# LayerNorm of a conformer convolution on eight Trainium2 cores: all spreads made at once, statistics in four row groups, residuals queued behind part of the next tile's normalisation, second projection's weight loads behind the relayout

## What is computed

```python
def conv_module(h, state, w_pw1, b_pw1, w_dw, b_dw, ln_g, ln_b, w_pw2, b_pw2):
    a, gt = jnp.split(h @ w_pw1 + b_pw1, 2, axis=-1)
    u = a * jax.nn.sigmoid(gt)                                   # GLU (B, T, D)
    up = jnp.concatenate([state.astype(u.dtype), u], axis=1)
    z = lax.conv_general_dilated(up, w_dw[:, None, :], ...) + b_dw
    z = jax.nn.silu(layer_norm(z, ln_g, ln_b))
    return z @ w_pw2 + b_pw2, up[:, T:]
...
x = x + g1[:, None, :] * y
h = modulate(rms_norm(x, p['norm_ffn'][i]), sh2, sc2)
```

## Time and profile before

| what | us |
|---|---|
| median of 3 runs (3391.39 to 3393.15) | 3391.57 |
| the profiled execution | 3392.49 |
| its span on the slowest core (core 5) | 3391.4 |
| spans of the eight cores | 3371.2 to 3391.4 |
| TensorE busy on core 5 | 3085.2 |

### The profile page before, as it was taken

One profiled execution on the slowest core, in us unless ns is written; L12 is line 12 of the kernel. 1 busy time (PEld: TensorE's weight loads), 2 busy tenths in 40 slices (PEclk: granted clock), 3 DMA queues, 4 the chain that ended last, 5 costly groups with the idle time before them and its releaser, 6 DMA issues.

```text
span 3391.4 us, 54958 instructions; the slowest of 8 cores (3371.2 to 3391.4 us)
## 1 busy us (share of the span) xinstructions
PE 3085.2 (91%) x22054; PEld 1831.1 (54%) x22054; DVE 1158.1 (34%) x2470; ACT 671.8 (20%) x1587; POOL 271.2 (8%) x391
## 2 busy tenths in 40 slices
PE   1299995797999999999999889989899999999997
PEld 0055552444555555555555445556566666666664
DVE  0543334424142213141222636652414414141417
ACT  1222223323000000000001546641300000000013
POOL 0000001001000000000000122410100000000000
PEclk9599996898999999999999999999899999999999
DMA  9956764244777877777752231214343444444443
GB/s 194 191 110 133 140 130 94 86 75 75 125 125 127 142 127 127 125 125 125 127 95 52 41 73 36 57 26 75 53 74 68 81 75 75 75 73 73 72 73 113
DMA packets 78139, 327.71 MB, mean 97 GB/s; under 512 B 19825, under 2 KB 39153, under 8 KB 43697
## 3 DMA queue, kind: packets, MB, share of 16 engines
q0 software_dynamic: 40432, 283.66, 47.7%
q1 hardware_dynamic: 37458, 40.54, 4.1%
HBM read 593.07 MB, written 10.19 MB: 178 GB/s over the span
## 4 chain that ended last, share of the span: by engine, by line
PE 85%; DVE 5%; DMA 3%; ACT 3%; issue 2%; SPq 2%; another core or an unknown queue 1%; POOL 0%; DVEq 0%; ACTq 0%; POOLq 0%
PE ps L308 85%; SPq L303 2%; DVE X L314 1%; DVE SCR L314 1%; ACT HB L311 1%; DMA X<-xT 1%; DVE X L317 1%; ACT SCR L311 1%; DVE SCR L681 1%; DMA RING<-wgu 1%; DMA UBraw<-UBraw 1%; POOL HB L693 0%; DMA kT_o<-UBraw 0%; DMA RING<-wpw 0%
## 5 line engine op out<-in xcount | busy, mean ns | idle before, releaser
L308 PE MATMUL ps<-HB,RING 128*128 128x384 bf16 (+2 forms) x11712 | 1946.0, 327 | 81.9 <-DVE X L317 20.7
L308 PEld LDWEIGHTS ps<-HB,RING 128*128 128x128 bf16 x11712 | 1140.4, 99 | 852.8 <-issue 159.5
L308 PE MATMUL ps<-UBraw,RING 128*128 128x384 bf16 (+3 forms) x5248 | 814.0, 313 | 1.8 <-DVE AMB L317 0.8
L308 PEld LDWEIGHTS ps<-UBraw,RING 128*128 128x128 bf16 x5248 | 492.7, 98 | 301.6 <-issue 19.2
L317 DVE SCALAR_TENSOR_TENSOR X<-ps,MOD,X 128x16 f32<-128x16 f32 (+2 forms) x1120 | 454.9, 447 | 469.9 <-PE ps L308 466.8
L314 DVE TENSOR_TENSOR UBraw<-ps,SCR 128x384 bf16<-128x384 f32 (+2 forms) x264 | 144.2, 547 | 1184.0 <-PE ps L308 1177.8
L311 ACT ACTIVATE SCR<-ps 128x416 f32<-128x416 f32 (+4 forms) x336 | 169.0, 504 | 1782.0 <-PE ps L308 1759.8
L311 ACT ACTIVATE SCR<-X 128x384 bf16<-128x384 f32 (+3 forms) x224 | 135.9, 609 | 260.0 <-DVE X L317 257.3
L308 PE MATMUL ps<-SCR,ONESB 128*128 128x384 bf16 (+3 forms) x336 | 87.7, 357 | 76.9 <-ACT SCR L311 73.1
L127 POOL DMA_DIRECT2D RING<-wgu x88 | 46.8, 531 | 1169.5 <-PE ps L308 1169.4
L311 ACT ACTIVATE SCR<-ps,UBraw 128x193 bf16<-128x193 f32 (+1 forms) x264 | 109.1, 419 | 90.7 <-DVE UBraw L1263 41.5
(11 more groups left out here) (91 smaller groups left out, 1058.9 us busy)
## 6 DMA issues: line engine op xcount, KB each, us to landing
RING<-wmod POOLq DMA_DIRECT2D x96, 1024.0 KB, 15.4
RING<-wgu POOLq DMA_DIRECT2D x88, 1024.0 KB, 8.9
RING<-wdn POOLq DMA_DIRECT2D x40, 1024.0 KB, 8.6
RING<-wpw POOLq DMA_DIRECT2D x24, 1024.0 KB, 15.4
RING<-wqkv POOLq DMA_DIRECT2D x10, 1024.0 KB, 9.0
X<-xT SPq DMA_DIRECT2D x4, 2368.0 KB, 55.2
RING<-wo POOLq DMA_DIRECT2D x8, 1024.0 KB, 8.8
X<-xT SPq DMA_DIRECT2D x8, 768.0 KB, 4.4
```

The lines of the kernel that those rows point to most:

```text
L308: return PE.emit(nc.tensor.matmul(out, lhsT=lhsT, rhs=rhs, start=start, stop=stop, **kw))
```

## The change

Five things are changed, all in the first layer's convolution module.

1. The load of `pw2_1` (and with it those of `pw2_2` and `pw2_3`, which stand behind it in POOL's queue) waits until the last relayout has landed.
2. The statistics lie in four groups of 296 frames, on all 128 rows, in place of three groups of 416 on 96 rows. The division by 2048 is in the ones (`ONESB`), and two one-element activations are queued so that ACT's tables for Sqrt and Silu are loaded at another place.
3. The spreads of all three tiles are queued in one go, in six pieces (a group of 296 frames can straddle a tile's border), to banks 5 and 6 for tile 0, 0 and 1 for tile 1, 2 and 3 for tile 2. PE waits for its own result after each piece. Tile 0's mean and reciprocal are read from PSUM by DVE; those of tiles 1 and 2 are copied by ACT, behind the first and the second Silu of tile 0.
4. At a tile's end 6 steps of the next tile's normalisation are queued ahead of the residuals of output blocks 0 to 5, and 5 steps between these and the residuals of blocks 6 and 7, in place of 3 ahead and 2 behind each residual.
5. For tile 2 only 4 output blocks are made in the common loop over k, and `pw2_0` and `pw2_1` are released after it; blocks 4 to 7 follow one by one. The waits for a tile's weights and banks stand ahead of its loop.

```diff
+        self.after = {}
...
-            self.pool.wait(self.free[s])
+            self.pool.wait(self.free[s], self.after.get(name))
...
-        MEAN = [MR0[:, 0, :], MR0[:, 1, :], MR2[:, 0, :]]
-        RSC = [MR0[:, 2, :], MR0[:, 3, :], MR2[:, 1, :]]
-        LST = carve(SCR, 9984, (128, 2, 416), F32)
+        MEAN = [PS[5], MR0[:, 0, :], MR0[:, 1, :]]
+        RSC = [PS[6], MR0[:, 2, :], MR0[:, 3, :]]
+        LST = carve(SCR, 9984, (128, 2, 296), F32)
...
-        DVE.emit(nc.vector.memset(ONESB[:], 1.0))
+        DVE.emit(nc.vector.memset(ONESB[:], 1.0 / D))
...
+        ring.after["pw2_1"] = (rl_sem[1], 16 * 4 * 8)
...
             for (bi, src) in ((5, ZB), (6, ZSQ)):
-                for t in range(3):
-                    mm(PS[bi][32 * t:32 * t + 32, 0:416], ONESB[:, 0:32], src[:, c % 2, TS[t]:TS[t] + 416], c == 0, c == KC - 1,
-                       tile_position=(0, 32 * t))
+                for j in range(4):
+                    mm(PS[bi][32 * j:32 * j + 32, 0:296], ONESB[:, 0:32], src[:, c % 2, 296 * j:296 * j + 296], c == 0, c == KC - 1,
+                       tile_position=(0, 32 * j))
...
+        act(CTs[:, 0, 0:1], EPSC[:], AF.Sqrt)
         DVE.wait(zs_pe[15])
-        q96 = slice(0, 96)
-        DVE.emit(nc.vector.tensor_scalar_mul(out=LST[q96, 0, :], in0=PS[5][q96, 0:416], scalar1=1.0 / D))
+        DVE.emit(nc.vector.tensor_copy(out=LST[:, 0, :], in_=PS[5][:, 0:296]))
...
-        stt(LST[q96, 1, :], PS[6][q96, 0:416], 1.0 / D, LST[q96, 1, :], ALU.mult, ALU.subtract)
...
+        tt(LST[:, 1, :], PS[6][:, 0:296], LST[:, 1, :], ALU.subtract)
...
+        act(LST[:, 1, :], LST[:, 1, :], AF.Sqrt, bias=EPSC[:, 0:1], scale=1.0)
         DVE.wait(ACT.tick())
-        DVE.emit(nc.vector.reciprocal(out=LST[q96, 1, :], in_=LST[q96, 1, :]))
+        act(CTs[:, 0, 1:2], EPSC[:], AF.Silu)
+        DVE.emit(nc.vector.reciprocal(out=LST[:, 1, :], in_=LST[:, 1, :]))
         t_lst = DVE.tick()
...
+        PIECES = [[(0, 0, 296, 0), (1, 0, 88, 296)], [(1, 88, 208, 0), (2, 0, 176, 208)], [(2, 176, 120, 0), (3, 0, 296, 120)]]
+        SPB = [(5, 6), (0, 1), (2, 3)]
+        sp_tok = {}
+        PE.wait(t_lst, t_sel)
+        for t in range(3):
+            for (j, lo, n, o) in PIECES[t]:
+                rows = slice(32 * j, 32 * j + 32)
+                for w_ in range(2):
+                    bi = SPB[t][w_]
+                    bank_wait(bi)
+                    mm(PS[bi][:, o:o + n], SEL[rows, :], LST[rows, w_, lo:lo + n], True, True, tile_position=(32 * j, 0))
+                    sp_tok[(t, w_)] = PE.tick()
+
+                PE.wait(PE.tick())
+
+        def ln_copy(t):
+            for w_ in range(2):
+                bi = SPB[t][w_]
+                ACT.wait(sp_tok[(t, w_)])
+                act((MEAN, RSC)[w_][t][:, 0:TN[t]], PS[bi][:, 0:TN[t]], AF.Identity)
                 bank_tok[bi] = [ACT.tick()]
...
-        ln_spread(0)
         lng_ = ln(0)
+        pump(lng_, 1)
+        ln_copy(1)
+        pump(lng_, 1)
+        ln_copy(2)
         pump(lng_, 40)
-        ln_spread(1)
-        ln_spread(2)
         for t in range(3):
             lng_ = ln(t + 1) if t < 2 else iter(())
+            wide = 6 if t < 2 else 4
+            w4 = [ring.use(f"pw2_{n}", PE) for n in range(wide // 2)]
+            for n in range(wide):
+                bank_wait(HEADB[n])
             for k in range(KC):
                 PE.wait(ln_tok[(t, k)])
-                for n in range(6):
...
+                for n in range(wide):
                     mm(PS[HEADB[n]][:, 0:TN[t]], w4[n // 2][:, k, 128 * (n % 2):128 * (n % 2) + 128], rhs0(k, t), k == 0, False)
...
-            pump(lng_, 3)
+            pump(lng_, 6)
             late = []
-            for n in range(6):
+            for n in range(wide):
                 late.append((n, resid(HEADB[n], 0, 0, n, t, tp, x_tok[(t, n // 4)])))
-                pump(lng_, 2)
...
-            w4[3] = ring.use("pw2_3", PE)
-            for n in (6, 7):
-                tp = proj_group(w4[3], n % 2, [(0, TN[t], rhs0)], t, HEADB[n - 6], n)
...
+            for n in range(wide, 8):
+                if n % 2 == 0:
+                    w = ring.use(f"pw2_{n // 2}", PE)
+                    pump(lng_, 5)
+                bi = HEADB[n - wide]
+                tp = proj_group(w, n % 2, [(0, TN[t], rhs0)], t, bi, n)
```

More of the change, by code:

```diff
@@ L467, in build_nc @@
             tt(ID32[:], ID32[:], MT[:, 32 * j:32 * j + 32], ALU.add)
-        ts2(MASK[:], FLAG[:], -1.0, 1e30, ALU.add, ALU.mult)
+        ts2(MASK[:], FLAG[:], -1.0, 1e33, ALU.add, ALU.mult)
         DVE.emit(nc.vector.tensor_scalar_mul(out=BQ8[:], in0=VTs[:, VO["bq"]:VO["bq"] + 16], scalar1=0.125))
@@ L485, in build_nc @@
         for ti, (a, b_) in enumerate(tiles0):
-            act(RSTD0[:, a:b_], PS[ti][:, 0:b_ - a], AF.Sqrt, bias=EPSC[:, 0:1], scale=1.0 / D)
+            act(RSTD0[:, a:b_], PS[ti][:, 0:b_ - a], AF.Sqrt, bias=EPSC[:, 0:1], scale=1.0)
             bank_tok[ti] = [ACT.tick()]
@@ L677, in norm_finish @@
             ACT.wait(PE.tick(), rsfree[t % 2])
-            act(RSTD[:, t % 2, 0:n], PS[nm.banks[t]][:, 0:n], AF.Sqrt, bias=EPSC[:, 0:1], scale=1.0 / D)
+            act(RSTD[:, t % 2, 0:n], PS[nm.banks[t]][:, 0:n], AF.Sqrt, bias=EPSC[:, 0:1], scale=1.0)
             bank_tok[nm.banks[t]] = [ACT.tick()]
@@ L806, in build_nc @@
         t_brow = POOL.tick()
+        act(CTs[:, 0, 0:1], EPSC[:], AF.Sqrt)
         DVE.wait(zs_pe[15])
-        q96 = slice(0, 96)
-        DVE.emit(nc.vector.tensor_scalar_mul(out=LST[q96, 0, :], in0=PS[5][q96, 0:416], scalar1=1.0 / D))
+        DVE.emit(nc.vector.tensor_copy(out=LST[:, 0, :], in_=PS[5][:, 0:296]))
+        bank_tok[5] = [DVE.tick()]
         sync(DVE)
-        tt(LST[q96, 1, :], LST[q96, 0, :], LST[q96, 0, :], ALU.mult)
+        tt(LST[:, 1, :], LST[:, 0, :], LST[:, 0, :], ALU.mult)
@@ L812, in build_nc @@
         sync(DVE)
-        stt(LST[q96, 1, :], PS[6][q96, 0:416], 1.0 / D, LST[q96, 1, :], ALU.mult, ALU.subtract)
[L814 to L818, removed]
+        tt(LST[:, 1, :], PS[6][:, 0:296], LST[:, 1, :], ALU.subtract)
+        bank_tok[6] = [DVE.tick()]
+        ACT.wait(DVE.tick())
+        act(LST[:, 1, :], LST[:, 1, :], AF.Sqrt, bias=EPSC[:, 0:1], scale=1.0)
@@ L832, in ln_spread @@
+        def ln_copy(t):
[3 more added lines that the diff above has]
+                act((MEAN, RSC)[w_][t][:, 0:TN[t]], PS[bi][:, 0:TN[t]], AF.Identity)
                 bank_tok[bi] = [ACT.tick()]
-            ln_st[t] = ACT.tick()
+            sp_tok[(t, 0)] = sp_tok[(t, 1)] = ACT.tick()
         ln_tok = {}
@@ L841, in ln @@
             cols = slice(TS[t], TS[t] + n)
-            DVE.wait(ln_st[t])
             tk = {}
@@ L845, in ln @@
                 if c < KC:
+                    DVE.wait(sp_tok[(t, 0)])
                     tt(X[:, c, cols], X[:, c, cols], MEAN[t][:, 0:n], ALU.subtract)
@@ L849, in ln @@
                     p = c - 1
-                    DVE.wait(tk[p])
+                    DVE.wait(tk[p], sp_tok[(t, 1)])
                     tt(X[:, p, cols], X[:, p, cols], RSC[t][:, 0:n], ALU.mult)
+                    if t == 0:
+                        bank_tok[5] = bank_tok[6] = [DVE.tick()]
                     ACT.wait(DVE.tick())
@@ L888, in build_nc @@
             if t == 2:
-                for b in range(3):
-                    ring.release(f"pw2_{b}", tp)
-            pump(lng_, 3)
+                ring.release("pw2_0", tp)
+                ring.release("pw2_1", tp)
+            pump(lng_, 6)
             late = []
-            for n in range(6):
+            for n in range(wide):
                 late.append((n, resid(HEADB[n], 0, 0, n, t, tp, x_tok[(t, n // 4)])))
-                pump(lng_, 2)
                 if n:
@@ L898, in build_nc @@
                     norm_sq(nm1, m, t, tok)
-            w4[3] = ring.use("pw2_3", PE)
-            for n in (6, 7):
-                tp = proj_group(w4[3], n % 2, [(0, TN[t], rhs0)], t, HEADB[n - 6], n)
-                late.append((n, resid(HEADB[n - 6], 0, 0, n, t, tp, x_tok[(t, 1)])))
+            for n in range(wide, 8):
[4 more added lines that the diff above has]
+                tp = proj_group(w, n % 2, [(0, TN[t], rhs0)], t, bi, n)
+                if t == 2 and n % 2 == 1:
+                    ring.release(f"pw2_{n // 2}", tp)
+                late.append((n, resid(bi, 0, 0, n, t, tp, x_tok[(t, n // 4)])))
                 m, tok = late.pop(0)
                 norm_sq(nm1, m, t, tok)
-            if t == 2:
-                ring.release("pw2_3", tp)
             m, tok = late.pop(0)
```

6 lines of the change are left out of this document (removed).

## The result

The changed kernel takes 3347.8 us (median of 4 runs, 3345.14 to 3350.97) against 3391.48 for the kernel before, run beside it (median of 4, 3390.37 to 3393.15): a ratio of 0.9869, 95% interval 0.9857 to 0.9881. It is 43.7 us faster; the forecast was 53.4.

A forecast was written before the change was run, and what follows sets the result against it. TensorE bounds the kernel, so time comes off where it idles or runs at half clock. The terms sum to 53.4 us off 3392.5, giving 3339 profiled and 3338 median; own range 3328 to 3347, 8 in 10 with 3355 as the top.

The forecast's parts named there:

- the slow relayout: Rival: the relayout's 720 small packets, not the weight loads, make its 17.79 us; 37.2 us off, 3354; chance 9%.
- relayout wait: TensorE's idle of 14.03 us before the last convolution, with the weight loads held: 13.5 us off.
- last convolution: The convolution behind the relayout stays at full clock after a shorter idle, 4.73 us against 7.39: 2.7 us off.
- statistics chain: The 7.99 us idle before the spread falls to 4.7 through shorter instructions and a moved table load: 3.3 us off.
- tile 0: From the spread's start to the end of tile 0's loop, 42.5 us becomes 30.5: 12.0 us off.
- tile 1 and its clock: Tile 1's gap and loop, idle down to 2.4 and no half clock, 35.75 us becomes 27.7: 8.0 off.
- tile 2 and its clock: Tile 2 and the way into the next projection, 49.6 us becomes 37.2: 12.4 off.
- clock in the new idles: Idles of 2.4 and 2.8 us before the loops of tiles 1 and 2 cost one clock fall: 2.5 us added.
- next projection: Its weights come in time, so its first 16 matmuls take 2.76 us and not 5.28: 2.5 off.
- All cores have these idles, and ... so the gain stays: Claim that the gain summed on core 5, 53.4 us, holds, as later TensorE work is unbroken and its weights in time.
- The gain is not given back: Denies the rival that later stages wait for weights that come no sooner, leaving 3391.5 us; chance 3%.
- The low clock: Rival: the clock falls in the new idles from tile 0's loop on; all low 3406 us, 4%; half low 3370, 3%.

The follow-up runs named there:

- e1: The kernel before with the held weight loads alone; 3375.06 to 3376.84 us in four runs, ratio 0.9955 to the kernel before.
- e2: The change without the held weight loads; 3361.35 us, ratio 0.9911 to the kernel before.
- e3: The change with ACT's copies for tiles 1 and 2 put back behind all 16 Silus of tile 0; 3352.43 us, one run.
- e5: The change with the ten normalisation instructions taken from ahead of residual 6, four of them between residuals 6 and 7; 3336.36 to 3339.66 us, ratio 0.9834.
- e4: The change with the old order of residuals, 3 normalisation steps ahead and 2 behind each of the first six; 3359.38 us, one run.
- e7: e5 with the spreads of tiles 1 and 2 later and tile 0's mean and reciprocal copied to SBUF; 3337.2 to 3339.44 us, a fifth run 3351.07.
- e6: The change with six output blocks in tile 2's common loop, as in the other tiles; 3348.31 and 3351.86 us, ratio 0.987.

## Why the prediction held, and where it was ten microseconds off

The direction held, and so did the account of what TensorE waits for. The forecast gain was 9.7 us too large. The forecast's own range ended at 3347, and the median lies 0.8 above it; that it lies inside the range to 3355 is luck, for the range was drawn that far for the slow relayout, which e1 rules out. Core 5's own stretch, term by term, beside the prediction's terms:

| term | forecast | core 5 | what it is in the trace |
|---|---|---|---|
| relayout wait | -13.5 | -14.2 | end of one convolution to the next 16.9, now 2.7 |
| last convolution | -2.7 | -1.2 | 7.4, now 6.2 |
| statistics chain | -3.3 | -3.3 | convolution's end to spread 11.2, now 7.9 |
| tile 0 | -12.0 | -11.6 | spread to loop 23.4, now 11.8; loop 19.0 in both |
| tile 1 and its clock | -8.0 | -6.4 | gap 15.3, now 9.4; loop 20.1, now 19.6 |
| tile 2 and its clock | -12.4 | -10.6 | gap 16.4, now 10.0; loop 22.0, now 15.0; way out 11.5, now 14.3 |
| clock in the new idles | +2.5 | in the two rows above | |
| next projection | -2.5 | -2.9 | to its end 111.1, now 108.2 |
| sum | -51.9 | -50.2 | 274.4, now 224.2 |

Two terms are missing in this table. The statistics matmuls, forecast at 1.5, lie ahead of the stretch: a block's take 0.43 us in place of 0.53, and the median block 22.14 in place of 22.23, about 1.3 for 14 blocks; the start of core 5's stretch came 0.9 earlier (527.3, now 526.4). And the tail of core 5 grew by 1.2. Core 5's span fell by 49.8 (3391.4, now 3341.6).

**What was right.** The relayout landed 2.3 us behind its last issue on seven cores and 3.8 on core 7, where I had taken about 3. An estimate by the Trainium skill (DMA: Bandwidth & Descriptors, "Anatomy of one DMA") was 2.2 for 80 KB; the trace agrees with it on the seven, though the page's fit is of DMAs that GpSimd issues, and these are SP's. The idle before the spread is 4.71 (4.7). The idles before the loops are 2.47 and 2.80 (2.4 and 2.8). The spread took 10.88 us (7.9 + 3.0 = 10.9), but that is luck, for its two parts were both wrong: the chain shows pieces of 2.32, 1.14, 1.73, 1.52, 1.19 and 2.32 us, 10.2 in all, and 0.14 between them, in place of 7.9 and 0.5. A short piece costs more for each column (1.14 for 176) than a long one (2.32 for 592), so each seems to have a fixed part of its own, which the price by columns left out. The statistics, too, came out at the forecast in part by another way: the cast that had slowed the product is later because of a DMA (e2).

**The first step that failed is "With an idle of 2.31 us instead of 14 the convolution behind it stays at full clock, 4.73 against 7.39".** It rested on one core, and on a row that could not tell: behind the idle of 2.31 stand 0.53 us of statistics matmuls at full speed, and then TensorE waited for 14 us. In the change the idle is 2.30 on every core; on six of eight the convolution takes 6.2 to 6.4 us, on cores 2 and 7 it takes 4.7. On core 0 the statistics matmuls still run at full speed, 0.43 us as on core 7, and the clock falls in the convolution behind them (timeline of PE, core 0):

```profile
521.34 0.43 PE L308 MATMUL ps<-SCR,ONESB 128*32 128x296 bf16 x8 [2.30 <-ACT SCR L311]
521.59 6.41 PE L308 MATMUL ps<-UBraw 128*32 128x312 bf16 x136
```

The windows of core 5 and of core 2 (columns as above):

```profile
530.00:534.00 4.00, 4.00 (x96) 3.08 (x88) 0.00 (x0) 1.32 (x4) 0.66 (x2) 0.73 0.69 109
```

```profile
534.00:537.00 3.00, 3.00 (x96) 2.62 (x92) 0.00 (x0) 1.32 (x4) 0.52 (x1) 1.00 0.58 101
```

The same idle ahead of the same work gave 0.73 on one core and 1.00 on another; and core 7 kept its clock although the 1.17 us for the relayout came on top. In e1 seven of eight cores stayed up, and e3 has cores where 2.80 left the clock alone. Over all cores the term is 1.0 (6.9, now 5.9), not 2.7.

**The second is "Each costs 0 or 2.5. I take one".** Both new idles cost, on every core, but about 1.6 each (1.4 to 1.7): 3.2 and not 2.5. e5 shows it as an experiment: with idles of 1 us the loops take 18.0 and 13.4, which are the values the prediction had without its clock term (18.3 and 13.4).

**The third, and the largest, is that the whole sum was made on core 5**, under "All cores have these idles, and ... so the gain stays". All have them, but not of one length. The stretches of the profiled executions, core 0 to 7:

| kernel | 0 | 1 | 2 | 3 | 4 | 5 | 6 | 7 | mean |
|---|---|---|---|---|---|---|---|---|---|
| before | 269.0 | 268.9 | 272.2 | 266.1 | 269.5 | 274.4 | 268.1 | 271.0 | 269.9 |
| change | 224.6 | 224.4 | 223.6 | 224.7 | 224.4 | 224.2 | 224.8 | 223.7 | 224.3 |

Core 5 had the longest stretch before: its wait for weights was the longest (3.52 us, 1.38 on the core with the shortest), so its way into the next projection took 11.5 us against 9.3 to 11.4 on the others, and the projection, begun at half clock, 111.1 against 108.2 on four of them. The change took that away: core 5's stretch fell by 50.2, the mean over the cores by 45.6. The mean span fell by 44.9 (3381.0, now 3336.1), near to what the time shows. That core 2 is the slowest now, with 3345.7 against core 5's 3341.6, is another matter: its stretch is 0.6 shorter than core 5's and fell by 48.6, but it starts 4.3 us later (530.7 against 526.4). Before, it started 1.8 later. The account closes: the forecast for the profiled execution was 3339.1, it took 3346.69, 7.6 more; 3.6 of that are core 5's own (53.4 against 49.8), 4.1 the other core's, and these lie ahead of the stretch, where the cores differ by some 14 us in both kernels (519.1 to 533.2 before, 517.1 to 530.7 now). The last 2.0 lie between profiled executions and medians: 3347.8 is 1.1 above its profile, where I had taken 0.9 below.

**The rivals.** The relayout is not slow by itself (e1). The gain is not given back: the tail is 2588.0 after 2586.4, and 2586 to 2588 in the experiments (2589 on the four cores of e4). The low clock did not last: by the Trainium skill (TensorE: Matmul & The Clock Gate, "A second HAM failure mode: psum-queue depth-cycling") short idles between groups make the clock go up and down, and it did go down, behind both of the longer ones; but between 566 and 572, 590 and 600, and 619 and 627 us the granted clock is 1.00 on core 5, so each loop lost some 1.6 us at its start, and the low clock did not hold for half of the stretch.

```profile
566.00:572.00 6.00, 6.00 (x39) 3.60 (x38) 1.64 (x4) 1.99 (x3) 0.00 (x0) 1.00 0.70 228
...
590.00:600.00 10.00, 10.00 (x63) 6.02 (x62) 3.95 (x8) 3.67 (x5) 0.00 (x0) 1.00 0.50 162
...
619.00:627.00 8.00, 8.00 (x48) 4.46 (x46) 0.00 (x0) 0.00 (x0) 0.00 (x0) 1.00 0.60 195
```

What decides whether one idle of 2.3 to 2.8 us takes the clock down on a given core was not settled.

## What to carry to other kernels

A short copy that stands on the path should not share the DMA engines with bulk loads that are needed later: hold the loads until the copy has landed, and count how long they have left. In an in-order queue put the work that frees a buffer ahead of the work that only has to be done sometime, and look for the remaining idle of 2 to 3 us too, since here it mostly cost its own length and then a stretch at half clock. Where a program runs on many cores, work a forecast out on several of them: here the slowest had more to win at the place being mended than the mean (50.2 against 45.6), and another core was the slowest afterwards.

## What the runs showed of the hardware that was not expected

**PSUM reads on DVE.** Tile 0's normalisation takes one operand from PSUM, and that costs nothing. The forecast was 0.52 us for each of 32 instructions; timeline of DVE, core 5, against the earlier trace rows:

```profile
539.22 0.47 DVE L314 TENSOR_TENSOR SCR<-SCR 128x296 f32<-128x296 f32 x1
...
546.50 15.05 DVE L314 TENSOR_TENSOR X<-X,ps 128x384 f32<-128x384 f32 x32 [3.51 <-PE ps L308]
```

15.05 / 32 is 0.47, as from SBUF (15.09). The Trainium skill (VectorE: DVE Perf Modes, "Rules for kernel authors") names a copy of the matmul's output to SBUF as the choice where many operations read it. The trace does not bear that out for these instructions: e7 makes the copy, and its 32 instructions take 15.09.

**A neighbour on POOL.** The statistics' product, 539.22 in the rows above, takes 0.47 for 296 columns alone and 1.46 beside POOL's cast (e2): an engine with hardly any work triples an instruction that lies on the path.

**Matmuls that do not lift the clock.** The fp32 spread keeps TensorE busy for 9.38 of 11 us, and the granted clock is 0.50 through all of it (windows, core 5). Moved into a gap (e7), it did not keep the clock up there either: 0.57 in the 4 us behind it.

```profile
544.00:555.00 11.00, 9.38 (x24) 5.79 (x23) 8.49 (x19) 3.58 (x7) 3.38 (x1) 0.50 0.32 68
```

**The clock is not decided by one idle.** In e3 it fell on core 3 behind the idle of 2.80, on cores 0, 2, 6 and 7 behind a later one of 1.22, on the other three behind neither; on core 6 of e6 an idle of 2.02 brought it down, and on core 7 of the change 2.30 and then 1.17 did not.
